# Reordering the opening of a transformer kernel: two small loads, a landing semaphore, eleven unread products and a square root

## The reference, cut to what matters

```python
def rmsnorm(x, g):
    y = x * lax.rsqrt(jnp.mean(x * x, axis=-1, keepdims=True) + EPS)
    return y * g

def swiglu(h, w_gate, w_up, w_down):          # 1024 -> 2816 -> 1024
    return (silu(h @ w_gate) * (h @ w_up)) @ w_down

x = x + 0.5 * swiglu(rmsnorm(x, ffn1_norm[0]), ffn1_w_gate[0], ffn1_w_up[0], ffn1_w_down[0])
... # later: memory_cross_attention(q_mem, rmsnorm(mem, mem_norm[0]), ...)
```

## Time and profile before

| | |
|---|---|
| time, median of 3 runs | 2104.94 us (2102.16 to 2106.1) |
| the profiled execution's own time | 2103.5 us |
| its span | 2101.3 us (2.2 us lie around it) |
| busy: TensorE / VectorE / ScalarE / GpSimd | 87% / 39% / 28% / 6% of the span |
| granted TensorE clock, mean | 0.93 of full |
| DMA | 603.69 MB, mean 287 GB/s |
| chain that ended last, by engine | TensorE 57%, DMA 40%, VectorE 2%, ScalarE 1% |

### The profile page before, as it was taken

One profiled execution on the slowest core, in us unless ns is written; L12 is line 12 of the kernel. 1 busy time (PEld: TensorE's weight loads), 2 busy tenths in 40 slices (PEclk: granted clock), 3 DMA queues, 4 the chain that ended last, 5 costly groups with the idle time before them and its releaser, 6 DMA issues.

```text
span 2101.3 us, 30715 instructions
## 1 busy us (share of the span) xinstructions
PE 1822.1 (87%) x13272; PEld 1355.3 (64%) x13272; DVE 810.9 (39%) x952; ACT 598.8 (28%) x704; POOL 130.4 (6%) x140
## 2 busy tenths in 40 slices
PE   8999999999999999999999986677777667667776
PEld 8999997999999998599999741122222112122221
DVE  7655557765665564766658600000000000000000
ACT  6333547533443354654427400000000000000001
POOL 4200011400000000220001000000000000000000
PEclk9999999999999999999999988797888888889788
DMA  8555552555555454156557999999999999999998
GB/s 273 180 180 165 159 182 94 186 180 184 197 185 190 153 185 138 41 186 226 180 171 258 404 427 428 428 428 428 428 428 429 429 428 429 429 428 429 429 428 344
DMA packets 182536, 603.69 MB, mean 287 GB/s; under 512 B 11952, under 2 KB 139440, under 8 KB 158016
## 3 DMA queue, kind: packets, MB, share of 16 engines
q1 hardware_dynamic: 180560, 601.43, 73.6%
q10 hardware_dynamic: 1648, 0.70, 0.1%
q0 software_dynamic: 256, 0.52, 0.1%
HBM read 601.58 MB, written 1.05 MB: 287 GB/s over the span
## 4 chain that ended last, share of the span: by engine, by line
PE 57%; DMA 40%; DVE 2%; ACT 1%; issue 0%; SPq 0%; ACTq 0%; POOL 0%; DVEq 0%; POOLq 0%
PE ps L1086 22%; DMA bulk<-in_w_up 19%; PE ps L1100 12%; DMA bulk<-in_w_down 10%; DMA bulk<-in_w_gate 10%; PE ps L1263 3%; PE ps L1704 2%; PE ps L1052 2%; PE ps L1157 1%; PE ps L1156 1%; PE ps L1158 1%; PE ps L1166 1%; PE ps L1168 1%; PE ps L1167 1%; PE ps L1285 1%; PE ps L1140 1%
## 5 line engine op out<-in xcount | busy, mean ns | idle before, releaser
L1086 PE MATMUL ps<-part,part 128*128 128x256 f32 x3840 | 460.1, 280 | 0.2 <-DVE part L2307 0.2
L1086 PEld LDWEIGHTS ps<-part,part 128*128 128x128 f32 x3840 | 455.5, 188 | 0.6 <-DVE part L2307 0.4
L1704 PE MATMUL ps<-bulk 128*32 128x512 f32 x1536 | 237.2, 751 | 158.7 <-DMA bulk<-in_w_up 100.5
L2307 DVE TENSOR_TENSOR part<-bulk,part 128x2048 fp32r<-128x2048 f32 x88 | 203.3, 2351 | 220.2 <-ACT part L1798 220.2
L1704 PEld LDWEIGHTS ps<-bulk 128*32 128x32 f32 x1536 | 48.6, 124 | 332.4 <-issue 127.1
L1100 PE MATMUL ps<-part,part 128*128 128x256 f32 x2112 | 255.5, 280 | 0.0
L1100 PEld LDWEIGHTS ps<-part,part 128*128 128x128 f32 x2112 | 251.8, 188 | 0.0
L1798 ACT ACTIVATE part<-bulk 128x2048 fp32r<-128x2048 f32 x86 | 160.1, 1911 | 226.2 <-DMA bulk<-in_ffn_w_up 226.2
L2963 DVE TENSOR_TENSOR keep<-keep,ps 128x512 f32<-128x512 f32 x16 | 11.0, 688 | 533.4 <-PE ps L1704 533.4
L1732 PE MATMUL ps<-bulk,keep 128*32 128x512 f32 x864 | 126.0, 715 | 33.1 <-DMA bulk<-in_w_down 32.6
L2316 DVE TENSOR_TENSOR part<-bulk,part 128x2048 fp32r<-128x2048 f32 x45 | 103.2, 2306 | 46.5 <-ACT part L1813 46.5
(11 more groups left out here) (336 smaller groups left out, 2368.1 us busy)
## 6 DMA issues: line engine op xcount, KB each, us to landing
bulk<-in_w_down SPq DMA_DIRECT2D x53, 2048.0 KB, 40.3
bulk<-in_w_gate SPq DMA_DIRECT2D x49, 2048.0 KB, 40.8
bulk<-in_w_up SPq DMA_DIRECT2D x47, 2048.0 KB, 40.2
bulk<-in_ffn_w_gate SPq DMA_DIRECT2D x44, 1024.0 KB, 5.5
bulk<-in_ffn_w_up SPq DMA_DIRECT2D x44, 1024.0 KB, 8.0
bulk<-in_ffn_w_down SPq DMA_DIRECT2D x44, 1024.0 KB, 5.3
keep<-in_w_up SPq DMA_DIRECT2D x17, 2048.0 KB, 40.7
keep<-in_w_gate SPq DMA_DIRECT2D x15, 2048.0 KB, 40.9
```

The costliest lines, as they stand in the source:

```text
L1086: ins = pe.matmul(y, w_, x_, start=(k == m == 0), stop=(k == KD - 1 and m == 2))
L1704: ins = pe.matmul(ps[j * CAP:(j + 1) * CAP, half, :], xe[:, k, :], w[:, kk, j * HALF:(j + 1) * HALF], start=(k == 0), stop=(k == KD - 1))
L2307: dve.tensor_tensor(hi(slot(3 * b + i)), slot(3 * b + i), as32(w_hi(f, b, i)), ALU.subtract).then_inc(gu_split, 1)
```

## The change

It touches the first 40 us of the program, in four places.

1. SyncE: gate 1 and up 1 are issued straight behind up 0; the constants follow them, and `alow_w` goes behind the memory rows.
2. Gate 1 gets a semaphore of its own, `gate1_loaded`. ScalarE splits gate 1 as soon as that has landed, and waits for up 1 only ahead of up 1's split. The counts that later waits on `gu_ready` compare with are lowered by 16 for both buffers in place of one.
3. TensorE makes three more products of `ident` with itself behind the transposes of half 0, and eight behind those of half 1, into bank 0, whose contents are overwritten.
4. ScalarE takes the root for `x` (which waits for `rsum_done`) ahead of the two squares of the memory rows (which wait for `mem_loaded`), not behind them.

```diff
@@ -756,7 +757,7 @@
         def gu_landed(eng, f, c, b):
             before, k = filled(f, c, b)
-            eng.wait_ge(gu_ready[b], 32 * (before + 1) - 16 * (b == 0) + k * 16)
+            eng.wait_ge(gu_ready[b], 32 * (before + 1) - 16 + k * 16)
@@ -777,7 +778,7 @@
                 for i, w in enumerate((wg, wu)):
                     src = w.rearrange("(k p) n -> p k n", p=P)[:, :, bass.ds(c * CW, CW)]
-                    landing = gate0_loaded if isinstance(c, int) and f == c == i == 0 else gu_ready[b]
+                    landing = (gate0_loaded, gate1_loaded)[c] if isinstance(c, int) and f == i == 0 and c < 2 else gu_ready[b]
                     sp.dma_start(slot(3 * b + i).rearrange("p (k n) -> p k n", k=KD), src).then_inc(landing, 16)
@@ -797,11 +798,11 @@
                 if f == 0:
                     gu_loads(0, 0, p)
+                    gu_loads(0, 1, 1 - p)
                     sp.dma_start(cst[:, P:NCONST], A["const"][:, P:NCONST]).then_inc(const_loaded, 16)
-                    sp.dma_start(alow_w, A["vecs"][:, NVA + NVB:NVEC].rearrange("p (k c) -> p k c", k=KD)).then_inc(alow_loaded, 16)
-                    gu_loads(0, 1, 1 - p)
                     dn_load(0, 0, p)
                     sp.dma_start(mem_rows, A["mem"][0].rearrange("(t p) d -> p t d", p=P)).then_inc(mem_loaded, 16)
+                    sp.dma_start(alow_w, A["vecs"][:, NVA + NVB:NVEC].rearrange("p (k c) -> p k c", k=KD)).then_inc(alow_loaded, 16)
                     dn_load(0, 1, 1 - p)
@@ -1298,6 +1299,8 @@
                     ins = pe.transpose(yT(k)[:, t * P:(t + 1) * P], xn[:, t, k * P:(k + 1) * P], ident)
                     if t and k % 2:
                         ins.then_inc(x_turned, 1)
+                for _ in range((3, 8)[t]):
+                    pe.matmul(bank(0)[:, 0:P], ident, ident, start=True, stop=True)
             ffn(0)
@@ -1792,9 +1795,15 @@
             def split_gu(f, c, b):

-                gu_landed(act, f, c, b)
+                first = isinstance(c, int) and f == 0 and c == 1
+                if first:
+                    act.wait_ge(gate1_loaded, 16)
+                else:
+                    gu_landed(act, f, c, b)
                 after(act, gu_used, f, c)
                 for i in range(2):
+                    if first and i == 1:
+                        gu_landed(act, f, c, b)
                     act.activation(hi(w_hi(f, b, i)), slot(3 * b + i), ACT.Copy).then_inc(gu_hi, 1)
@@ -1831,13 +1840,13 @@
                 if f == 0:
                     act.wait_ge(const_loaded, 16)
                     act.activation(small[:, 251:252], epsc, ACT.Sqrt)
+                act.wait_ge(rsum_done, f + 1)
+                root(bank(4)[:, 0:T])
+                if f == 0:
                     act.wait_ge(mem_loaded, 16)
                     for t in range(TT):
                         act.activation(memT[:, 4 * t:4 * t + 4, :], mem_rows[:, t, :], ACT.Square,
                                        accum_out=small[:, 18 + t:19 + t]).then_inc(mem_ssq, 1)
-                act.wait_ge(rsum_done, f + 1)
-                root(bank(4)[:, 0:T])
-                if f == 0:
                     act.wait_ge(mem_ssq, 2)
                     act.activation(small[:, 18:20], small[:, 18:20], ACT.Sqrt, bias=epsc, scale=1.0 / D).then_inc(mem_ssq, 1)
```

More of the change, by code:

```diff
@@ L250, in program @@
         gate0_loaded = sem("gate0_loaded")
+        gate1_loaded = sem("gate1_loaded")
         gate0_half = sem("gate0_half")
```

## The result

| | before | changed |
|---|---|---|
| time, median of 22 runs each | 2102.66 us (2101.18 to 2106.1) | 2105.86 us (2104.12 to 2109.57) |
| the profiled execution's own time / span | 2103.5 / 2101.3 us | 2108.07 / 2105.9 us |

The ratio is 1.0016, 95% interval 1.001 to 1.0022: 3.2 us slower on the median, 0.16%. That is less than the 0.2% which the prediction called no change, yet the interval of 22 runs of each leaves no change out.

What follows compares the result with a forecast made beforehand. TensorE was taken to bound the kernel, its opening's gains or losses standing unchanged in the end time. 2.4 us (mean) + 1.7 (clock) = 4.1 slower, on 2104.2, gave 2108.3 us; range 2102.8 to 2110.8.

Steps and rivals of the forecast that it cites:

- The mechanism: In the opening, VectorE's subtractions and GpSimd's sums take turns; the mean comes late, 4.1 us slower in all.
- the pause: VectorE's 3.80 us idle ahead of gate 1, where sums two and three ran; the change was to close it.
- The wait: TensorE, behind 24 products of chunk 1, was to wait 3.8 us for the mean, until 30.4.
- The shift by the three products: Unread products behind half 0 were to move half 1's start and what follows by 1.05 us.
- the term of 2.4 us for the mean: The mean's product on TensorE was to stand 2.4 us later than before (27.98), delaying everything behind it there.
- The clock: TensorE's wait was to bring one stretch at 1.2 GHz, costing 1.7 us, bounded by 0.5 and 2.9.
- Loads: Gate 1 was to land at 16.2 and up 1 at 19.15, both 1.4 us earlier; down 0 at 24.4.
- Root ahead of the memory squares: ScalarE's reordering in the opening was to be worth 0 and cost 0; TensorE wants the memory rows at 36.5.
- Strictly by issue: Rival, chance 0.18: VectorE and GpSimd get shared access in order of issue; mean 0.1 us later than before, 2104.3 us.
- No collision: Rival, chance 0.12: gate 1 lands late or GpSimd's sums slip through; TensorE never waits, 1.0 us gained, 2103.2 us.
- The clock that stays low twice as long: Rival, chance 0.12: TensorE's clock falls twice or stays low longer, 2.4 + 2.9; 2109.5 us, or 2110.5.
- the unread products alone: Holding TensorE's clock in chunk 0 was to give nothing by itself, since split gate 1 comes at 24.8 anyhow.

Runs made afterwards that it cites:

- the wait that was added: The changed kernel with VectorE's subtraction for up 1 made to wait for GpSimd's last sum; median 2102.37 us, ratio to before 1.0001.
- the sums' move: The changed kernel with the first four sums on VectorE, between the subtractions for gate 1 and up 1, not on GpSimd; median 2101.79 us, ratio to before 0.9998.
- the filled one: The changed kernel with twelve more unread products on TensorE ahead of its wait for the mean; median 2105.59 us, ratio to before 1.0014.

## Why the prediction was right, point by point

**The time and the sign.** 2105.86 lies in the range, and slower by 3.2 us was measured where 4.1 was summed. That the forecast of 2108.3 lies 2.4 us too high has two parts: 0.9 is the effect, and 1.5 is that I counted from 2104.2, the mean of four times, where 22 runs have a median of 2102.66. That sum and median agree to 0.9 us is in part luck: in the two profiles the first down product stands 3.8 and 5.0 us later than before, the median loses 3.2, and no run here shows how often the clock falls for how long.

**The mechanism** was the forecast's own. The step that carries it, that a subtraction and a sum take turns and that the change closes the pause, is shown by the wait that was added (3.5 us back) and by the sums' move. The turns came in the order that the prediction lists: first sum, gate 1, second sum, up 1, third sum, down 0, last sum. The last sum was worked out to end at 30.35 and ended at 29.79; the mean's product was to stand at 30.4 and stood at 29.93. The wait was put at 3.8 us and was 3.07.

**Terms that were mis-sized.** The shift by the three products: 0.6 us (half 1 at 7.97), not 1.05, since half 1 ran partly at the full rate (8 transposes in 1.44 us where half 0 needed 1.97). With it the sums began at 16.62, not 17.3, and the term of 2.4 us for the mean became 1.95 (29.93 less 27.98, by the chain of waits of either kernel; 2.11 by TensorE's timelines, where the product before stands at 27.82). The clock: 1.7 was summed; the two profiles show 2.5 and 1.2 us on the 48 products (8.52 and 7.18, less 6.01) and 0.5 to 0.6 on the mean's (1.19, less 0.67 or 0.60), but the medians give 1.1 between the changed kernel and the filled one. My bounds of 0.5 and 2.9 were near. That an idle time of 1.92 us brings a low stretch, from which the term was taken, is no rule: ahead of the mean's product 2.10 and 2.17 us brought none.

**What the sum did not part.** The three products moved all behind half 1, and the prediction has this in its 2.4 us. It did not ask what the loads and the semaphore would do without them: a wait of 2.1 us, no fall of the clock and a first down product 0.9 to 1.0 us late. Of the 3.8 and 5.0 us that the two profiles of the changed kernel lost at that product, the larger part came with the products, which were to win time.

**Loads.** They came 0.6 to 1.0 us earlier than worked out: by issue and time to landing, gate 1 landed at 15.5 (3.25 and 12.3 us), up 1 at 18.5 (6.70 and 11.8) and down 0 at 23.4 (12.51 and 10.9), where 16.2, 19.15 and 24.4 were said.

**Costs put at nothing.** Constants and `alow_w`: right, no reader waited for them. Root ahead of the memory squares: TensorE found the memory rows ready in every profile here; with products and root alone nothing moved. VectorE took up gate 1 at 19.42, 0.8 us before I had it, and that too went into the wait.

**The rivals.** Strictly by issue: the mean would have stood at 28.1; it did not. No collision: fell. The clock that stays low twice as long was given 0.12 as a case of its own; it happened in the first profile and not in the second, so it is one of the ways in which executions of one kernel differ. My statement that the unread products alone would not pay, since gate 1 was due at 24.8 anyhow, is what products and root alone show.

## What to carry to other kernels

An idle stretch on one engine may be the only time in which another can work. Before a pause is closed, look up in its stretch who runs in it, and whether that one's instructions take longer wherever the first engine is busy; here a sum took 1.30 us in VectorE's pause and 3.2 us outside. Where the two must meet, let the one that is waited for first go first, or move its work to the engine that holds the place. The move is no gain by itself: in the kernel before, where the pause was still there, the sums on VectorE made TensorE wait 1.17 us.

## What the hardware showed that I had not expected

- **Who wins a turn.** In no profile with the sums on GpSimd did the first sum run between the subtractions for gate 0 and up 0. In the changed kernel it was issued at 16.62, 0.4 us ahead of the second of them (17.02), and still took 3.85 us, which spans the rest of the first and the whole second; the later ones each waited for one subtraction only. The Trainium skill ("SBUF — State Buffer", "Who interferes with whom") gives the turn to the one issued first. The runs agree with it from the second sum on and not for the first; why, no run here settles.
- **A low clock of two lengths.** Behind an idle time of 3.07 and 3.05 us the same kernel's clock was low for over 6.6 us once and for 3.2 to 3.4 once; behind 2.58 us, in the kernel with VectorE's sums and no products, for 6.7 us. Nor does the length of the idle time alone say whether it falls: 1.92 us ahead of chunk 0 brought a low stretch in the kernel before, 2.10 and 2.17 us ahead of the mean's product brought none. On one execution a stretch is 1.7 to 3 us, as much as the whole change.
